# VectorE sums the second layer's last modulation third during the first FFN

## What is computed

```python
c_act = jax.nn.silu(c)
for l in range(DEPTH):
    mod = (c_act @ w_mod[l] + b_mod[l])[:, None, :]
    sh1, sc1, g1, sh2, sc2, g2 = jnp.split(mod, 6, axis=-1)
    h = rmsnorm(x, norm1_g[l]) * (1.0 + sc1) + sh1
    proj = h @ w_in[l]
    # attention, convolution and state-space branch, each projected, gated, summed: mixed
    x = x + g1 * (mixed @ w_out[l])
    h2 = rmsnorm(x, norm2_g[l]) * (1.0 + sc2) + sh2
    gu = h2 @ w_ffn_in[l]
    f_gate, f_up = jnp.split(gu, 2, axis=-1)
    x = x + g2 * ((jax.nn.silu(f_gate) * f_up) @ w_ffn_out[l])
```

## Time and profile before

| what | value |
|---|---|
| median of 3 runs | 954.51 us (954.43 to 958.81) |
| profiled execution | 955.28 us, its span 953.4 us |
| TensorE busy | 909.9 us (95% of the span) |
| VectorE busy | 710.3 us (74%) |
| ScalarE busy | 480.8 us (50%) |
| chain that ended last | PE 56%, DVE 25%, DMA 6%, ACT 5%, issue 5% |
| DMA | 196.09 MB, mean 206 GB/s |
| w_mod loads | 48 of 1 MB, median 6.0 us to landing |
| modulation blocks on TensorE (line 656) | 288 matmul records, median 617 ns, overlapping |
| accumulations on VectorE (line 1694) | 10, mean 2346 ns |

### The profile page before, as it was taken

The page is one execution under the profiler, slowest core; times in us unless marked ns, Lnnn a source line. Parts: engine busy times, 40 slices in busy tenths (PEclk is TensorE's granted clock), DMA queues, the critical chain, the costliest instruction groups (busy, mean ns, idle before and its releaser), DMA issues.

```text
span 953.4 us, 15556 instructions
## 1 busy us (share of the span) xinstructions
PE 909.9 (95%) x6523; PEld 762.5 (80%) x6523; DVE 710.3 (74%) x940; ACT 480.8 (50%) x598; POOL 15.1 (2%) x15
## 2 busy tenths in 40 slices
PE   5889999999999989999999999999999999999996
PEld 1788976767778889899988998677777888888884
DVE  3883989998577677775767679889957766666666
ACT  4684158724637455546355325693274544343434
POOL 2000000000000000000000000000000000000002
PEclk9999999999999999999999999999999999999998
DMA  8973366668696458866885534444969555555621
GB/s 356 239 251 129 128 222 221 221 163 292 258 301 227 137 176 295 317 202 222 277 297 126 185 134 133 132 133 133 299 231 337 194 160 193 200 177 188 198 100 44
DMA packets 128628, 196.09 MB, mean 206 GB/s; under 512 B 30793, under 2 KB 90705, under 8 KB 122415
## 3 DMA queue, kind: packets, MB, share of 16 engines
q1 hardware_dynamic: 128247, 195.03, 61.6%
q10 hardware_dynamic: 312, 0.08, 0.0%
HBM read 194.02 MB, written 1.06 MB: 205 GB/s over the span
## 4 chain that ended last, share of the span: by engine, by line
PE 56%; DVE 25%; DMA 6%; ACT 5%; issue 5%; SPq 2%; ACTq 0%; DVEq 0%
PE bank L618 12%; PE bank L619 11%; PE bank L620 11%; PE bank L963 8%; DVE wlo L1520 7%; DVE yc L1815 5%; PE bank L964 4%; DMA raw<-in_w_mod 3%; ACT whi L1154 3%; DMA raw<-in_w_in 2%; PE bank L722 2%; PE bank L656 1%; PE bank L889 1%; PE bank L849 1%; PE bank L746 1%
## 5 line engine op out<-in xcount | busy, mean ns | idle before, releaser
L1520 DVE TENSOR_TENSOR wlo<-raw,whi 128x2048 fp32r<-128x2048 f32 (+1 forms) x136 | 302.7, 2227 | 174.0 <-PE bank L620 80.4
L1154 ACT ACTIVATE whi<-raw 128x2048 fp32r<-128x2048 f32 x132 | 251.0, 1909 | 118.0 <-DMA raw<-in_w_in 39.1
L618 PE MATMUL bank<-hb,whi 128*128 128x256 f32 x592 | 170.8, 289 | 1.4 <-DVE wlo L1520 1.2
L619 PE MATMUL bank<-hb,whi 128*128 128x256 f32 x592 | 167.8, 283 | 0.2 <-issue 0.2
L620 PE MATMUL bank<-hb,wlo 128*128 128x256 f32 x592 | 167.6, 283 | 0.0
L618 PE MATMUL bank<-whi,bhi 128*128 128x512 f32 x304 | 121.6, 400 | 2.9 <-DVE wlo L1520 2.9
L963 PE MATMUL bank<-hb,whi 128*128 128x512 f32 x336 | 119.0, 398 | 0.0
L619 PE MATMUL bank<-wlo,bhi 128*128 128x512 f32 x304 | 118.8, 391 | 0.0
L620 PE MATMUL bank<-whi,blo 128*128 128x512 f32 x304 | 118.7, 390 | 0.0
L618 PEld LDWEIGHTS bank<-hb,whi 128*128 128x128 f32 x592 | 113.7, 192 | 4.8 <-DVE wlo L1520 2.2
L619 PEld LDWEIGHTS bank<-hb,whi 128*128 128x128 f32 x592 | 113.7, 192 | 0.8 <-issue 0.4
(11 more groups left out here) (273 smaller groups left out, 1117.6 us busy)
## 6 DMA issues: line engine op xcount, KB each, us to landing
raw<-in_w_mod SPq DMA_DIRECT2D x48, 1024.0 KB, 6.0
raw<-in_w_ffn_in SPq DMA_DIRECT2D x44, 1024.0 KB, 5.2
raw<-in_w_in SPq DMA_DIRECT2D x38, 1024.0 KB, 7.2
raw<-in_w_ffn_out SPq DMA_DIRECT2D x22, 1024.0 KB, 5.0
raw<-in_w_out SPq DMA_DIRECT2D x8, 1024.0 KB, 8.3
raw<-in_w_in SPq DMA_DIRECT2D x16, 256.0 KB, 4.5
raw<-in_ssm_glu_b SPq DMA_DIRECT2D x4, 1024.0 KB, 6.4
raw<-in_ssm_glu_a SPq DMA_DIRECT2D x4, 1024.0 KB, 5.2
```

Source lines behind the costliest of these rows:

```text
L618: mm(o, w_hi, a_hi, start=start, stop=False, skip_group_check=True)
L619: mm(o, w_hi, a_lo, start=False, stop=False, skip_group_check=True)
L1154: fn(whi[mi % N_HI][:, :], raw[SLOT[item]][:, :], ACT.Copy).then_inc(s_hi, 1)
L1520: part = V.tensor_tensor(wlo[mi % N_LO][:, n], raw[SLOT[("main", *divmod(mi, NB))]][:, n], whi[mi % N_HI][:, n].bitcast(F32), ALU.subtract)
```

## The change

Third 2 of the second layer is no longer multiplied by TensorE block by block in that layer's mixing. Its eight blocks are loaded in the first layer and summed by VectorE at steps 24, 30, 31, 34, 35, 38, 40 and 43 into the upper half of `blx`, which is idle then. Third 0's sums move from steps 41, 42, 43, 44, 46, 47 to 41, 42, 44, 45, 46, 47. `blx` is needed later, so the sum goes to DRAM: ahead of the load of the first layer's block 46, SyncE waits for the eighth sum and stores 1 MB to `summed`; ScalarE waits for that store before it writes this half of `blx`. In the second layer the sum is loaded back as one modulation block (1, 2, 8), ahead of step 29, and multiplied by ones. The stores and loads of gate and bias that hung on the old blocks now stand ahead of main blocks 27 and 29.

```diff
--- before.py
+++ after.py
@@ -157,15 +157,18 @@
 
 NORM_MODS = 2
 MOD_AT = {0: {5 + 3 * (n // 2) + n % 2: (1, n) for n in range(DK)} | {19 + 3 * (n // 2) + n % 2: (2, n) for n in range(DK)}}
-MOD_AT[1] = {i: m for i, m in MOD_AT[0].items() if m[0] == 2}
+SUMMED = DK
+MOD_AT[1] = {29: (2, SUMMED)}
 
 BEFORE_NORM = (AT[("wo", 3)], NB - 1)
 
 MIX_TURN_AT = {2 * AT[("cp", 1)] + 1: (0, 1), 2 * AT[("wo", 0)]: (2,), 2 * AT[("wo", 0)] + 1: (3,)}
 
 PREP_AT = AT[("fg", 1)]
-ACC_AT = {i: (1, ng, NORM_MODS + n) for ng, places in enumerate(((41, 42, 43, 44, 46, 47), (53, 56, 58, 59, 61, 62)))
-          for n, i in enumerate(places)}
+ACC_PLACES = {2: (24, 30, 31, 34, 35, 38, 40, 43), 0: (41, 42, 44, 45, 46, 47), 1: (53, 56, 58, 59, 61, 62)}
+ACC_AT = {i: (1, ng, DK - len(places) + n) for ng, places in ACC_PLACES.items() for n, i in enumerate(places)}
+ACC_AT = {i: ACC_AT[i] for i in sorted(ACC_AT)}
+KEEP_AT = 46
 SUM_AT = {49: (1, 0), 64: (1, 1)}
 
 ROUNDS = 2 * STEPS + 2
@@ -209,7 +212,7 @@
         return [3] if SUM_AT[i] == (1, 0) else []
     if (l, i) == (1, 0):
         return [4]
-    return [3 * m[0] + m[1] for m in mods_at(l, i) if m[2] == DK - 1] if i >= 0 else []
+    return [3 * m[0] + m[1] for m in mods_at(l, i) if m[2] in (DK - 1, SUMMED)] if i >= 0 else []
 
 
 def used(mi):
@@ -238,6 +241,7 @@
 ITEMS, SLOT, LANDED, AFTER = plan_loads()
 
 ACC_NO = {("mod", *m): n for n, m in enumerate(ACC_AT.values())}
+ACC_END = {ng: ACC_NO[("mod", 1, ng, DK - 1)] + 1 for ng in range(3)}
 PE_MODS = [x for x in ITEMS if x[0] == "mod" and x not in ACC_NO]
 
 
@@ -249,7 +253,7 @@
     return PE_MODS.index(item) + sum(PE_MODS.index(item) >= 3 * DK + NORM_MODS for _ in SUM_NO)
 
 
-MOD_ENDS = [DK, 2 * DK, 3 * DK, SUM_NO[0] + 1, SUM_NO[1] + 1 + NORM_MODS, SUM_NO[1] + 1 + NORM_MODS + DK]
+MOD_ENDS = [DK, 2 * DK, 3 * DK, SUM_NO[0] + 1, SUM_NO[1] + 1 + NORM_MODS, SUM_NO[1] + 1 + NORM_MODS + 1]
 LO_NO = {}
 for _e in ("pool", "dve"):
     for _n, _m in enumerate([(l, i) for l in range(DEPTH) for i in range(NB) if lo_engine(i) == _e]):
@@ -321,7 +325,7 @@
         uc = sb("uc", [P, CT, PAD + T])
         yc = sb("yc", [P, CT, T])
         qT = h[:, 0:4, :]
-        modacc = h[:, :, :].rearrange("p a b -> p (a b)")
+        modacc = [h[:, :, :].rearrange("p a b -> p (a b)")] * 2 + [blx[:, 2048:4096]]
         kT = sb("kT", [P, T])
         vv = sb("vv", [P, 3, P])
         rtmp = m[:, 0:2, :]
@@ -395,6 +399,7 @@
         s_land = [sem(f"raw_landed{n}") for n in range(N_RAW)]
 
         s_hi, s_unit, s_modused, s_modacc = sem("hi_ready"), sem("unit_ready"), sem("mod_weights_used"), sem("mod_accumulated")
+        s_kept = sem("sum_kept")
         s_lo = {"pool": sem("lo_ready_pool"), "dve": sem("lo_ready_dve")}
 
         s_dve, s_act = sem("dve_step"), sem("act_step")
@@ -461,6 +466,7 @@
             kind, n = NAMES[i]
             return 2 * n - 1 + (kind == "fu")
 
+        summed = nc.dram_tensor("summed", (P, MODC), F32, kind="Internal").ap()
         gate_row = nc.dram_tensor("gate_row", (2 * DEPTH, D), F32, kind="Internal").ap()
         def x_final(n, p):
 
@@ -574,16 +580,31 @@
                 dst, landed, _ = landed_in(item)
                 if item[0] == "mod":
                     _, l, ng, k = item
-                    if k in (4, 6) and ng == 2:
+                    if k in (4, 6) and (l, ng) == (0, 2):
                         (store_gate, spread_gate)[k // 6](sp, l, 1)
                     if k in (4, 6) and l and ng == 0:
                         (store_gate, spread_gate)[k // 6](sp, l - 1, 2)
-                    if k == 6 and (l, ng) != (0, 0):
+                    if k == 6 and (l, ng) not in ((0, 0), (1, 2)):
 
                         sp.wait_ge(mod_tr, 3 * l + ng)
                         load_bias(sp, l, ng)
-                    sp.dma_start(dst, A["w_mod"][l, k * P:(k + 1) * P, ng * MODC:(ng + 1) * MODC]).then_inc(landed, 16)
+                    if k == SUMMED:
+                        sp.wait_ge(s_kept, 16)
+                        src = summed
+                    else:
+                        src = A["w_mod"][l, k * P:(k + 1) * P, ng * MODC:(ng + 1) * MODC]
+                    sp.dma_start(dst, src).then_inc(landed, 16)
                 else:
+                    if item[1:] == (0, KEEP_AT):
+
+                        sp.wait_ge(s_modacc, ACC_END[2])
+                        sp.dma_start(summed, modacc[2]).then_inc(s_kept, 16)
+                    if item[1:] == (1, 27):
+                        store_gate(sp, 1, 1)
+                    if item[1:] == (1, 29):
+                        spread_gate(sp, 1, 1)
+                        sp.wait_ge(mod_tr, 5)
+                        load_bias(sp, 1, 2)
                     if item[1:] == (0, AT[("gc", 3)]) and DEPTH > 1:
 
                         sp.wait_ge(gl_read, 4)
@@ -647,23 +668,24 @@
                 pe.wait_ge(landed, value)
                 if (l, ng, k) == (0, 0, 0):
                     pe.wait_ge(c_ready, 1)
-                elif k == 0 and (l, ng) != (1, 1):
+                elif k == (SUMMED if (l, ng) == (1, 2) else 0) and (l, ng) != (1, 1):
 
                     pe.wait_ge(mod_ready, 3 * l + ng)
                     if (l, ng) == (0, 1):
                         pe.wait_ge(bc_cp, ROUNDS)
                 for q in range(4):
-                    last = mm(b_mod[32 * q:32 * q + 32, :], cact32[:, k, :], weights[:, q * 512:(q + 1) * 512],
-                              start=(k == 0 and (l, ng) != (1, 1)), stop=(k == DK - 1 or (l, ng, k) == (1, 1, NORM_MODS - 1)), skip_group_check=True)
+                    last = mm(b_mod[32 * q:32 * q + 32, :], ones[:, 0:32] if k == SUMMED else cact32[:, k, :], weights[:, q * 512:(q + 1) * 512],
+                              start=(k in (0, SUMMED) and (l, ng) != (1, 1)), stop=(k in (DK - 1, SUMMED) or (l, ng, k) == (1, 1, NORM_MODS - 1)),
+                              skip_group_check=True)
                 last.then_inc(s_modused, 1)
 
             def mod_sum(l, ng):
 
-                pe.wait_ge(s_modacc, (DK - NORM_MODS) * (ng + 1))
+                pe.wait_ge(s_modacc, ACC_END[ng])
                 if ng:
                     pe.wait_ge(mod_ready, 3 * l + ng)
                 for q in range(4):
-                    last = mm(b_mod[32 * q:32 * q + 32, :], ones[:, 0:32], modacc[:, q * 512:(q + 1) * 512],
+                    last = mm(b_mod[32 * q:32 * q + 32, :], ones[:, 0:32], modacc[ng][:, q * 512:(q + 1) * 512],
                               start=(ng == 1), stop=(ng == 0), skip_group_check=True)
                 last.then_inc(s_modused, 1)
 
@@ -1217,6 +1239,8 @@
                 src = round_bank(l, n)[:, :]
                 if n >= 2:
                     a, t = divmod(n - 2, STEPS)
+                    if l and (a, t) == (1, 0):
+                        act.wait_ge(s_kept, 16)
                     fn(bl[:, a, t], src.rearrange("p (c n) -> p c n", c=CT), ACT.Copy).then_inc(bc_cp, 1)
                 else:
                     if n == 0:
@@ -1680,18 +1704,21 @@
                 item = ("mod", l, ng, k)
                 weights, landed, value = landed_in(item)
                 w = cact[:, k:k + 1]
-                if k == NORM_MODS:
-                    if ng == 0:
+                o = modacc[ng]
+                if k == DK - len(ACC_PLACES[ng]):
+                    if ng == 2:
+                        dve.wait_ge(at_hi, l)
+                    elif ng == 0:
                         dve.wait_ge(hhi_ready, H0["fg"] + DK)
                         dve.wait_ge(bc_src, 2 * l + 2)
                     else:
                         dve.wait_ge(ca_ready, 2 * l + 2)
                     dve.wait_ge(landed, value)
-                    last = V.tensor_scalar(modacc, weights, w, None, ALU.mult)
+                    last = V.tensor_scalar(o, weights, w, None, ALU.mult)
                 else:
                     dve.wait_ge(landed, value)
                     dve.wait_ge(s_modacc, ACC_NO[item])
-                    last = V.scalar_tensor_tensor(out=modacc, in0=weights, scalar=w, in1=modacc, op0=ALU.mult, op1=ALU.add)
+                    last = V.scalar_tensor_tensor(out=o, in0=weights, scalar=w, in1=o, op0=ALU.mult, op1=ALU.add)
                 last.then_inc(s_modacc, 1)
 
             def root(n, t):
```

## The result

The changed kernel took 971.8 us (median of 4 runs, 967.2 to 973.1), the kernel before 956.6 us on the same chip (954.4 to 958.8). The ratio is **1.0156, 95% interval 1.0136 to 1.0176**: slower, 2.3 us above the forecast of 969.5 and inside its range. Of these 2.3 us, 2.0 are the kernel before: the forecast stood on its median of 954.51, which a fourth run raised to 956.55. As a difference the forecast is 15.0 us, measured are 15.2. A later set of runs gave 1.0172 [1.0156, 1.0189], that is 16.7 us. The profiled execution of the changed kernel took 967.22 us, span 965.3. It is the quickest of all eight; the others have a lower mean granted clock (0.982 to 0.985 for its 0.990), that is more time at half clock. So the trace shows 11.9 us of the 15.2 between the medians.

The account below looks back on a forecast made before the run. TensorE was taken to bound the second FFN, VectorE part of the second layer's mixing. Terms 4.15 + 1.4 + 1.4 + 2.3 + 0.4 + 9.2 - 3.8 = 15.05 us gave 969.5 us; 8-in-10 range 959 to 976.

Parts of the forecast that it names:

- (0,2,5): First layer, ahead of gc 3: this block's load waits for gc 3's buffer; TensorE idles 4.9 us, net 4.15.
- The sums: First layer, VectorE: sum at 31 delays the norm 1.4 us, 35 delays fg 2's low part 2.3, 38 costs 0.4.
- The store: First layer, fu 4 and fo 3: SyncE's wait and the store delay fo 3's load; 9.2 us lost.
- The clock: TensorE at half clock after the idle before gc 3: 1.4 us lost, bounds 0 and 2.8.
- The second layer: Second layer's mixing: removed modulation blocks gain 3.8 us, limited by VectorE at gc 3; bounds 2.7 to 6.1.
- Rival (a): First layer, block 46 (fo 3): the store does not hold its load; 960.3 us, chance 0.15.
- (b): First layer, gc 3: conv's chain ends earlier and hides the late (0,2,5); 964 us, chance 0.11.
- Rival (c): First layer's additions are absorbed, second layer's gain stands alone; 950.7 us, at best 948.4, chance 0.06.
- (e): Second layer: removed loads change nothing, VectorE bounds it; 973 us at most, counted within the forecast's chance of 0.56.
- (d): More is late: other FFN loads, a second half-clock stretch, sums with no cover; about 976 us, chance 0.12.

Follow-up runs that it names:

- the changed kernel's second trace: The changed kernel unedited, run again on another chip beside runs of the kernel before: 971.7 us, ratio 1.0172; span of this trace 969.5 us.

## Why the prediction was right

**(0,2,5).** Right in place, cause and size. The load is issued 0.04 us after the low part of gc 3 ends, and the idle is 4.10 us for 4.9, as the load took 4.8 us and the wait for (0,2,4) ahead had already used 0.6 of it (the two together 4.7). That small wait I had not seen. The sum at 29 removes both.

**The sums.** 1.3 and 2.3 us where 1.4 and 2.3 were predicted, read off VectorE's order alone: the time from the end of one instruction to the start of the one that TensorE waits for, less the sum. The 0.4 us at 38 are 0.2: not at the low part, but one round later, in the wait of 2.90 us for 2.65. Moving 35 to 33 removed its wait, and against the changed kernel's second trace, which has half clock in fg 3 as well, it gives the 2.3 us back for good.

**The store.** The mechanism is right in all its parts. On the clock of before, fo 3's load is issued at 384.66 - 8.20 = 376.46 (376.4 predicted) and landed 7.4 us later (7.9 predicted); the idle is 6.49 us. The low part of fo 3 is 8.7 us late on that clock (396.28 - 8.20 for 379.4) and TensorE 8.8, for 9.2. The half clock behind the idle (2.3 of the 8.8) cost nothing beyond this, as predicted: it fills the time up to the second late copy, and with the sum at 42 TensorE, partly at half clock too, comes out 4.2 us late, just what the low part is. The experiments part the price: 4.5 us for the sum at 43 rather than 42, 2.5 for the transfer (shown with one row). The 1.8 left are what the wait for the sum still costs at 42, by subtraction.

**The clock.** I took one half-clock stretch of 1.4 us, and behind (0,2,5) it cost 1.5. A second, as long, came behind the idle of 2.60 us ahead of fg 2, which I had not weighed; by luck it came where the wait in fg 3 gave 1.4 us of it back. By the medians this is the term that is too small: in the second trace half clock came behind that wait instead and cost 1.3 us net, and the clock of the eight executions says that the profiled one had the least of it.

**The second layer.** 3.3 us for 3.8. At gc 3 TensorE was 2.7 us earlier (2.65 predicted). The last blocks gave 1.5 us where I had added 1.19, and 0.85 was lost again at 737 us, to a wait for VectorE that I had not looked at. No wait for the store or for the sum's load appeared, as I had costed them. The wait at gc 1 for the conv variance (1.67 us) was not foreseen either and costs nothing of its own: it takes the time that the low part of gc 3 would have taken. In the second trace of the changed kernel half clock ahead of it took that time instead (the wait there is 0.08 us), and TensorE waits 1.47 us for the low part of gc 3 in both.

**The sum.** 14.5 us for 15.05 in the trace, with small errors of both signs: the store 0.4 too high, the second layer's gain 0.5 too high, the half clock at fg 2 left out and all but given back. Against the medians it is 15.0 for 15.2 and, in the later set, 16.7. That it comes within 0.2 us is luck: the waits are a little shorter than forecast and the half clock longer, and where that falls changes from one execution to the next by more than this. Rival (a), the store harmless, and (b), the late row hidden, are shown wrong in the trace and became true only by edit. Rival (c), faster, names the right bound: the second layer's gain alone is a ratio of 0.9966, which also shows (e), no gain there, wrong. Of (d) the second half-clock stretch came.

## What to carry to other kernels

Moving work out of a late stretch is worth what that stretch's other engines let through: here 3.3 us of the 7 blocks' 6.9. Where loads go in order through a ring of buffers, one more item shifts who waits for whom for all behind it, and a wait put on the issuing queue delays every load behind the waiting one; both could be read here from the issue times before the change was made. When a sum is moved, check its loads, the waits of the engine that adds, and its reader: the third was forgotten here and cost 10.9 us.

## What the runs showed of the hardware

A 1 MB store just ahead of a 1 MB load on the same queue lengthened that load from 5.0 to 7.4 us to the start of its use. Of four 1 MB loads issued within 5 us, the second took 9.2 us until its use. Half clock came behind idles that cost little by themselves. Behind the 2.6 us ahead of fg 2's low part it followed in seven of eight traces. At the wait in fg 3 it followed in all five that waited 2.9 us there and in none of the seven that waited 1.5 to 1.7, all of which had had it at fg 2; with 2.65 us it followed in one trace and not in another. Behind the wait of 1.6 to 1.7 us at 601 to 621 us, the same in every kernel, it followed in six of fourteen. The profiled run of the changed kernel and its median differ by 4.6 us (967.2 and 971.8 us), at mean granted clocks of 0.990 and 0.984; that the clock is the whole of it is not shown.
